# Scores of two heads side by side, and projections in threes, in a stick-breaking attention

## The reference

```python
z = einsum('bhqd,bhkd->bhqk', qb, k) * scale           # scores
strict = key_idx < q_idx                                # keys before the query only
log_one_minus = where(strict, log_sigmoid(-z), 0.0)
suffix = cumsum(log_one_minus, reverse=True) - log_one_minus
w = where(strict, exp(log_sigmoid(z) + suffix), 0.0)
out = einsum('bhqk,bhkd->bhqd', w, v)
```

## Time and profile before

| | |
|---|---|
| time, median of 3 runs | 1234.1 us (1234.05 to 1234.74) |
| the profiled execution's own time | 1235.34 us |
| its span, first to last instruction | 1233.5 us |
| granted TensorE clock, mean | 0.993 of full speed |
| TensorE busy | 1199.7 us, 97% |
| VectorE, ScalarE, GpSimd busy | 57%, 41%, 7% |
| stick-breaking stage | from 101.2 us to about 274 us of the span |

### The profile page before, as it was taken

How to read it: one execution, slowest core, us unless ns; L and a number is a source line. 1 busy time by engine, 2 the same in 40 slices (tenths; PEclk the granted TensorE clock), 3 DMA queues, 4 the chain that set the end, 5 groups by cost and what they waited for, 6 DMA issues and landing times.

```text
span 1233.5 us, 15994 instructions
## 1 busy us (share of the span) xinstructions
PE 1199.7 (97%) x6548; PEld 964.2 (78%) x6548; DVE 701.2 (57%) x1086; ACT 500.9 (41%) x799; POOL 92.3 (7%) x72
## 2 busy tenths in 40 slices
PE   7999999999999999999999999999999999999996
PEld 5787777777777787887777788878888888888885
DVE  6644564359556676457887785364444444433356
ACT  5424434454454455224446545253233223322244
POOL 0390010104000000000000200000000000000000
PEclk9999999999999999999999999999999999999998
DMA  9732322213121343331112101123322222433322
GB/s 370 282 109 71 125 92 84 69 59 101 52 69 52 97 142 98 105 120 45 59 54 84 34 4 36 52 86 103 103 89 100 99 89 98 144 99 100 104 86 71
DMA packets 35593, 118.22 MB, mean 96 GB/s; under 512 B 3936, under 2 KB 6112, under 8 KB 35520
## 3 DMA queue, kind: packets, MB, share of 16 engines
q1 hardware_dynamic: 33024, 111.03, 26.9%
q0 software_dynamic: 1392, 4.72, 1.3%
q10 hardware_dynamic: 1104, 1.45, 0.3%
HBM read 112.99 MB, written 4.19 MB: 95 GB/s over the span
## 4 chain that ended last, share of the span: by engine, by line
PE 85%; DVE 6%; ACT 5%; issue 2%; POOL 0%; DVEq 0%; ACTq 0%
PE pb L650 82%; PE pb L906 1%; DVE wlo L1824 1%; PE pb L736 1%; ACT mP L1539 1%; DVE mnm L2066 1%; DVE xT L1824 1%; ACT whi L1341 1%; ACT Y L1341 1%; DVE mP L2056 1%; DVE junk L1835 0%; PE pb L1068 0%; ACT xT L1560 0%; DVE sp L1824 0%; ACT fv L1341 0%
## 5 line engine op out<-in xcount | busy, mean ns | idle before, releaser
L650 PE MATMUL pb<-hlo,whi 128*128 128x512 f32 (+2 forms) x1056 | 408.9, 394 | 7.1 <-DVE wlo L1824 5.9
L650 PE MATMUL pb<-hhi,wlo 128*128 128x512 f32 (+2 forms) x1056 | 410.8, 389 | 2.6 <-DVE wlo L1824 2.6
L650 PE MATMUL pb<-hhi,whi 128*128 128x512 f32 (+2 forms) x1056 | 409.9, 388 | 0.0
L1824 DVE TENSOR_TENSOR wlo<-raw,whi 128x1024 fp32r<-128x1024 f32 (+1 forms) x178 | 216.1, 1219 | 109.0 <-ACT whi L1341 108.0
L650 PEld LDWEIGHTS pb<-hlo,whi 128*128 128x128 f32 (+1 forms) x1056 | 198.5, 188 | 55.2 <-DVE wlo L1824 8.6
L650 PEld LDWEIGHTS pb<-hhi,wlo 128*128 128x128 f32 (+1 forms) x1056 | 198.1, 188 | 44.0 <-DVE wlo L1824 3.5
L650 PEld LDWEIGHTS pb<-hhi,whi 128*128 128x128 f32 (+1 forms) x1056 | 198.1, 188 | 41.0
L1341 ACT ACTIVATE whi<-raw 128x1024 fp32r<-128x1024 f32 (+1 forms) x178 | 181.5, 1034 | 72.9 <-PE pb L650 67.9
L650 PE MATMUL pb<-alo,whi 128*128 128x512 f32 x176 | 68.5, 389 | 0.0
L650 PE MATMUL pb<-ahi,wlo 128*128 128x512 f32 x176 | 68.5, 389 | 0.0
L650 PE MATMUL pb<-ahi,whi 128*128 128x512 f32 x176 | 68.5, 389 | 0.0
(11 more groups left out here) (363 smaller groups left out, 1632.6 us busy)
## 6 DMA issues: line engine op xcount, KB each, us to landing
raw<-w_all SPq DMA_DIRECT2D x173, 512.0 KB, 3.5
adab<-ada_d SPq DMA_DIRECT2D x12, 512.0 KB, 12.5
raw<-w_all SPq DMA_DIRECT2D x10, 384.0 KB, 3.0
xT<-xn_d SPq DMA_DIRECT2D x4, 512.0 KB, 12.9
gbt<-ada_d SPq DMA_DIRECT2D x4, 512.0 KB, 15.7
ple_scratch<-zs SPq DMA_DIRECT2D x8, 256.0 KB, 12.2
xT<-x_d POOLq DMA_DIRECT2D x8, 256.0 KB, 3.2
out_d<-xT SPq DMA_DIRECT2D x6, 256.0 KB, 2.6
```

The costliest lines, as they stand in the source:

```text
L650: return e.matmul(out, lhs, rhs, start=start, stop=stop, skip_group_check=True)
L1824: return e.tensor_tensor(out, a, b, op)
```

## The change

Scores are computed for a pair of heads at once. `qp` shrinks from 8 slices with zeros to 4 full slices: the even head's queries on partitions 0 to 63, the odd head's on 64 to 127. `sb_qk(pr)` multiplies 64 rows of `kp` with 64 rows of `qp`, one head after the other on different rows and into different banks, and adds the eight masks at the end. GpSimd's zeros and its share of the low part go away; VectorE makes the whole low part, 896 and 256 columns. The order on all engines is written anew: behind the scores of a pair stand three projections, then one behind each suffix, none behind `sb_pv`. The middle one of each group of three uses bank 6. The root and the scaling of the `kv` latent move from F6 to F8, and the four `Silu` of the first gate (with two table loads) move ahead of the three projections of the last pair.

```diff
-        QPE, KPE, SBV = sig("act_qp", range(8)), ...
+        QPE, KPE, SBV = sig("act_qp", range(4)), ...
+        def filler_bank(i):
+            return 6 if i % 5 == 1 else 7
@@ GpSimd
-            def sb_low(h):
-                ...
-                e.tensor_tensor(spl[:, 0:896], sp[:, h % 2, 0:896], fr(sph[:, 0:896]), ALU.subtract).then_inc(SBLO0.sem, 1)
-            for r in range(2):
-                ...
-                e.memset(qp[64 - 64 * r:128 - 64 * r, :, :].rearrange(...)[:, :, r, :], 0.0).then_inc(QZERO.sem, 1)
-            for h in range(8):
-                sb_low(h)
-                if h == 1:
-                    rope_sum("kr", krs[64:96, :], 0)
+            rope_sum("kr", krs[64:96, :], 0)
@@ TensorE
+            def sb_qk(pr):
+                ...
                 for kb in KB_ORDER:
-                    out = sb_out(h, kb)
-                    bank(3 * (h % 2) + BK[kb])
-                    mm(out, kp[:, h // 2, 128 * kb:128 * kb + 128], qp[:, h, 128 * kb:512], kb != 3, False)
-                    t = mm(out[:, 0:128], identB, msB, False, False)
-                t.then_inc(SBQK.sem, 1)
+                    for r in range(2):
+                        bank(3 * r + BK[kb])
+                        rows = slice(64 * r, 64 * r + 64)
+                        mm(sb_out(r, kb), kp[rows, pr, 128 * kb:128 * kb + 128], qp[rows, pr, 128 * kb:512], kb != 3, False)
+                for r in range(2):
+                    for kb in KB_ORDER:
+                        t = mm(sb_out(r, kb)[:, 0:128], identB, msB, False, False)
+                    t.then_inc(SBQK.sem, 1)
...
-            sb_qk(0)
-            next(fa)
             for pr in range(4):
                 h = 2 * pr
-                sb_qk(h + 1)
-                next(fa)
+                sb_qk(pr)
+                for _ in range(3):
+                    next(fa)
                 sb_suffix(h)
-                next(fa)
-                if pr < 3:
-                    sb_qk(h + 2)
                 next(fa)
                 sb_suffix(h + 1)
                 next(fa)
                 sb_pv(pr)
-                if pr < 3:
-                    next(fa)
@@ ScalarE
-                for r in range(2):
-                    copy(qp[64 * r:64 * r + 64, 2 * m + r, :], PB[m][64 * r:64 * r + 64, :], scale=0.125
+                copy(qp[:, m, :], PB[m][:, :], scale=0.125).then_inc(QPE.sem, 1)
...
-            sb_pre(0)
-            sb_pre2(0)
-            next(fa)
             for pr in range(4):
                 h = 2 * pr
-                next(fa)
+                sb_pre(h)
+                sb_pre(h + 1)
+                sb_high(h)
                 if pr == 3:
                     ... (load Silu table, 4 Silu, load the other table)
+                for _ in range(3):
+                    next(fa)
+                sb_high(h + 1)
                 sb_weights(h)
-                ...
                 next(fa)
                 sb_weights(h + 1)
                 next(fa)
@@ VectorE
+            def sb_low(h):
+                V.wait_ge(*SBHI(h))
+                if h:
+                    V.wait_ge(*SBSUF(h - 1))
+                for o, n in ((0, 896), (1024, 256)):
+                    t = tt(spl[:, o:o + n], sp[:, h % 2, o:o + n], fr(sph[:, o:o + n]), ALU.subtract)
+                t.then_inc(SBLO.sem, 1)
...
             for pr in range(4):
                 h = 2 * pr
-                ...
+                sb_pre(h)
+                if pr == 0:
+                    conv("cq", 0)
+                sb_pre(h + 1)
+                sb_max(h)
                 next(fa)
+                sb_max(h + 1)
+                sb_low(h)
                 next(fa)
+                next(fa)
+                sb_low(h + 1)
                 next(fa)
                 next(fa)
```

More of the change, by code:

```diff
@@ L241, in build @@
         with ExitStack() as s1:
-            qp = sb(s1, "qp", [128, 8, S])
+            qp = sb(s1, "qp", [128, 4, S])
             kp = sb(s1, "kp", [128, 4, S])
@@ L433, in build @@
         ZPLE = sig("act_zple", range(8))
[L435 to L439, removed]
+        QPE, KPE, SBV = sig("act_qp", range(4)), sig("dve_kp", range(4)), sig("act_sbv", range(4))
+        SBQK, SBMIN, SBLN, SBMAX, SBHI, SBLO, SBSUF = (
+            sig(n, range(8)) for n in ("pe_sbqk", "dve_sbmin", "act_sbln", "dve_sbmax", "act_sbhi", "dve_sblo", "pe_sbsuf"))
         SBW = sig("act_sbw", [(h, b) for h in range(8) for b in range(3)])
@@ L770, in tensor_program @@
             for m in range(4):
-                free[m] = [QPE(2 * m + 1)]
+                free[m] = [QPE(m)]
             for m in range(4):
@@ L780, in filler_a @@
                 for m in range(5):
-                    project(*(("cq", m) if m < 3 else ("ckv", m - 3)), 128, 7, h1)
-                    free[7] = [CQ(m)]
+                    b = filler_bank(m)
+                    project(*(("cq", m) if m < 3 else ("ckv", m - 3)), 128, b, h1)
+                    free[b] = [CQ(m)]
                     if m == 3:
@@ L791, in filler_a @@
                 yield
-                T.wait_ge(*SS(("c", 4)))
-                sum_squares(6, "kv", ssq[:, :])
                 for m in range(8):
-                    project(*(("sz", m) if m < 4 else ("mz", m - 4)), 128, 7, h1)
-                    free[7] = [ZE(m)]
+                    b = filler_bank(6 + m)
+                    if m == 2:
+                        T.wait_ge(*SS(("c", 4)))
+                        sum_squares(6, "kv", ssq[:, :])
+                    project(*(("sz", m) if m < 4 else ("mz", m - 4)), 128, b, h1)
+                    free[b] = [ZE(m)]
                     yield
                 for m in range(6):
-                    b = 0 if m == 4 else 7
+                    b = filler_bank(14 + m)
                     project("ga", m, 128, b, h1)
@@ L825, in sb_suffix @@
                        sp[:, i, 896:1024], False, False)
-                T.wait_ge(*SBLO0(h))
-                T.wait_ge(*SBLO1(h))
+                T.wait_ge(*SBLO(h))
                 for kb in range(3):
@@ L1446, in filler_a @@
                 yield
-                A.wait_ge(*CQN(2))
-                root(rsb[:, :], 6, 256, "kv")
                 for m in range(8):
                     conv(*(("sz", m) if m < 4 else ("mz", m - 4)))
+                    if m == 2:
+                        A.wait_ge(*CQN(2))
+                        root(rsb[:, :], 6, 256, "kv")
                     yield
@@ L1467, in sb_pre, with sb_high @@
                 e.activation(x, x, ACT.Ln, bias=one_c).then_inc(SBLN.sem, 1)
-            def sb_pre2(h):
+            def sb_high(h):
                 A.wait_ge(*SBMAX(h))
@@ L1476, in sb_weights @@
                 A.wait_ge(*SBSUF(h))
-                A.wait_ge(*SBLO0(h))
-                A.wait_ge(*SBLO1(h))
+                A.wait_ge(*SBLO(h))
                 for b, n in THIRDS:
@@ L1510, in scalar_program @@
             A.wait_ge(*SBPV(3))
-            A.wait_ge(*SBLO0(7))
+            A.wait_ge(*SBLO(7))
             for k in range(5):
@@ L1968, in filler_a @@
                     V.wait_ge(*PLST(7))
-                    e.tensor_copy(zs[:, m, :], PB[7][:, :]).then_inc(ZE.sem, 1)
-                    if m == 0:
+                    e.tensor_copy(zs[:, m, :], PB[filler_bank(6 + m)][:, :]).then_inc(ZE.sem, 1)
+                    if m == 2:
                         latent_normed("kv", 3, 2, V_KN)
@@ L1989, in sb_pre, with sb_max @@
                 t.then_inc(SBMIN.sem, 1)
-            def sb_pre2(h):
+            def sb_max(h):
                 V.wait_ge(*SBLN(h))
@@ L2015, in vector_program @@
                 V.wait_ge(*SBPV(pr))
[L2016 to L2020, removed]
+                e.tensor_copy(qp[:, pr, :], PB[6][:, :]).then_inc(OA.sem, 1)
             for m in range(4):
@@ L2023, in vector_program @@
                 V.wait_ge(*OA(m))
-                tt(zs[:, m, :], zs[:, m, :], qp[:, 2 * m, :], ALU.mult).then_inc(ZA.sem, 1)
+                tt(zs[:, m, :], zs[:, m, :], qp[:, m, :], ALU.mult).then_inc(ZA.sem, 1)
             next(fa)
```

36 lines of the change are left out of this document (4 added, 32 removed).

## The result

The changed kernel took 1245.4 us (median of 5 runs, 1242.6 to 1247.9) beside 1234.7 us of the kernel before (5 runs, 1234.1 to 1236.6): ratio 1.0076, 95% interval 1.0061 to 1.0092, so 10.7 us at the medians, where 8.8 were forecast. Its profiled execution took 1245.4 us, with a span of 1243.6 against 1233.5.

A forecast was written before the change was run, and what follows sets the result against it. TensorE, busy 97% of the span, bounds the kernel. Gains of 14.6 us against costs of 17.6 give 3.0 us more, plus 5.8 for the clock: 8.8 on 1234.1, so 1242.9 us; range 1239 to 1247, for 8 in 10 1236 to 1248.5.

The forecast's parts named there:

- Waits for low parts: TensorE waits for `wlo` ahead of F2 3.28, F3 0.3, F6 4.8, F7 3.28, F9 0.5 and F17 4.2 us.
- the two behind a suffix: Short waits for low parts ahead of F3, 0.3 us, and F9 (`sz 3`), 0.5 us.
- Scores by pairs: Two heads' scores on two halves of rows take 2.79 us instead of 5.04; gain 4 x 2.25 = 9.0 us.
- lost in the first pair for banks 3 to 5: First pair's second head waits for banks until ScalarE's copies of the values leave them: 0.8 us.
- Scores and fewer starts behind other work: Scores by pairs gain 9.0 us; projections starting behind other work fall from 20 to 13, gain 0.6 us.
- Old waits: TensorE's present waits in the stage, about 101 to 281 us, go: 5.0 us gained if none stayed.
- The clock: Granted clock falls behind each long wait, F2, F6, F7 and F17: four times 1.45 us, 5.8 us, bounds 0 and about 12.
- slow first steps: Each projection behind one of the four long waits pays 0.1 us for its first step: 0.4 us.
- VectorE's whole low part: VectorE's low part on all columns, at most 1.6 us twice a pair, behind at least one projection: worth nothing.
- The rival that hoped for a quicker VectorE: VectorE's chain ahead of F2, F6, F7, F17 shorter without GpSimd, each wait 2 us less: 1229.1 us, chance 0.10.
- the one in which the halves run apart: Scores on the two halves of rows don't run together, the 9.0 us are missing: 1251.9 us, chance 0.07.
- The rival with an unchanged clock: The waits come but the granted clock stays: 1234.1 + 3.0 = 1237.1 us, chance 0.14.

The follow-up runs named there:

- second experiment: Changed kernel with ScalarE and VectorE converting two weight chunks ahead everywhere, also where ada chunks lie between: 1227.05 us, ratio 0.9926 to the kernel before.
- third: Changed kernel with the four Silu and their two table loads behind ScalarE's three conversions of the last pair: 1237.1 us, ratio 1.0014 to the kernel before.
- ninth: Changed kernel with ScalarE's first conversion between the two heads' exponentials and logarithms from the second pair on: 1232.75 us, ratio 0.9971 to the kernel before.
- last experiments: Against the kernel with everything that waited mended (1218.0 us): 64-row scores one head after the other, 1225.0 us; zero-padded scores over all 128 rows, 1228.6 us.
- first experiment: Changed kernel with 14, 21, 14 and 18 identity products on TensorE ahead of F2, F6, F7 and F17: 1236.4 us, ratio 1.0011 to the kernel before.
- fourth experiment: Changed kernel with GpSimd again making the first 896 columns of each low part, VectorE the last 256: 1244.1 us, ratio 1.0056 to the kernel before.
- half-filled kernel: Changed kernel with 7, 11, 7 and 9 identity products on TensorE ahead of F2, F6, F7 and F17: 1241.1 us, ratio 1.0044 to the kernel before.
- filled kernel: Same run as the first experiment: changed kernel with identity products on TensorE in the four long waits, 1236.4 us.
- all-in kernel: Changed kernel with two weight chunks ahead, Silu block behind the three conversions, values' projection in banks 2, 5, 6, 7: 1218.0 us, ratio 0.9857 to the kernel before.

## Why the prediction was right, step by step

- **Waits for low parts.** Right in place, releaser and size, six of six: 16.4 us foretold, 16.3 measured in the same count (16.6 if the two behind a suffix also go from start to start). The second experiment shows their cause, the third and ninth the part that ScalarE's order has in F17 and F6.
- **Scores by pairs.** 2.79 us a pair as read from FoX, and 0.75 us lost in the first pair for banks 3 to 5 where 0.8 was foretold. The last experiments split the gain: 1.60 of 2.25 us a pair is the alternation of halves.
- **Scores and fewer starts behind other work.** The third pair, which has no stops in either kernel, takes 238.46 - 200.30 = 38.16 us from scores to scores against 238.48 - 197.90 = 40.58: 2.42 us, times four 9.7, as 9.0 + 0.6 foretold. After, then before:

```profile
200.30 2.43 PE L633 MATMUL pb<-qp,kp 64*128 64x512 f32 x16
...
238.46 2.43 PE L633 MATMUL pb<-qp,kp 64*128 64x512 f32 x16
```

```profile
197.90 1.02 PE L650 MATMUL pb<-qp,kp 128*128 128x512 f32 x2
...
238.48 1.02 PE L650 MATMUL pb<-qp,kp 128*128 128x512 f32 x2
```

- **Old waits.** Right that they go, but too small by 1.2 us. The prediction took them at 5.0 us, the idle time in brackets, and the new long ones from start to start. From start to start the seven old stops are 6.2 us (each stretch less the time that the same work takes without a stop: 2.52 us for scores, 2.79 for a suffix, 2.30 for a product with values).
- **The clock.** Right in kind, all four stops bring it down; mis-sized. The term was four times 1.45 us, 5.8, taken from the stretch of 2.93 us in the earlier trace rows; it measured 9.6, because three of the four stretches at 1.2 GHz lasted about twice as long as that one. That the total came out only 1.9 us over the 8.8 forecast is in part luck: the clock cost 3.8 us more than foretold, the old waits gave 1.2 more, and 1.6 came back far behind the stage. The rule of the Trainium skill (TensorE: Matmul & The Clock Gate, "Why this matters for your kernels"), that idle gaps between bursts bring the clock down, was borne out for all four. The 1.79 us gap at 57.54 alone would have misled: it was one draw, and in the first experiment's execution a gap of that length brought the clock down.
- **The sum.** All from start to start, -9.7 + 0.75 - 6.2 + 16.6 + 9.6 + 0.5 for slow first steps makes 11.55 us for a stage that grew by 11.3. The 0.3 us between weren't traced.
- **VectorE's whole low part** took 1.42 us and cost nothing, as priced. The rival that hoped for a quicker VectorE is refuted by the fourth experiment, and the one in which the halves run apart by the 2.79 us. The rival with an unchanged clock is what the first experiment made. It was worked out as 3.0 us slower than the kernel before. By the ratio it is 1.4 us slower (0.1 to 2.7), and its stage is 170.3 - 168.5 = 1.9 us longer; the old waits of 1.2 us too little account for the difference of the stages.

## What to carry to other kernels

When two steps are moved next to each other, ask what the step between them was hiding: here a copy, a sum and a conversion of 3.28 us in a row, hidden by 2.5 to 3 us of other work. On a kernel in which TensorE is busy 97% of the time, a stop costs its length and then the slow stretch behind it, here about 60% again (9.6 us on 16.3). Mend the look-ahead together with the new order: the order alone gave 1245.4 us and the look-ahead alone 1233.0, both together 1227.1. The last step to 1218.0 took the later Silu block and the free banks as well.

## What was not expected of the hardware

- A stop of 3.1 to 4.5 us was followed by 3.4 to 6.1 us in which products took nearly twice their time, costing 1.65 to 2.9 us each.
- Stops of 1.6 to 2.1 us bring the clock down at one time and not at another. In one execution of the half-filled kernel one of 2.13 us did, while 1.60, 1.60 and 2.11 us, and one of 2.07 us ahead of the stage, did not. At the same place ahead of the stage the clock fell in the filled kernel's execution (1.79 us) and stayed at 1.00 in those of the kernel before (1.79 us) and of the changed one (1.87 us). Ten executions of the half-filled kernel spread over 8 us, with a mean granted clock of 0.988 for the slowest and 0.995 for the fastest; but the kernel before, without long stops in the stage, spread over 4.8 us too (19 runs), and the all-in kernel's four within 1.3.
- Beside a subtraction on GpSimd, one on VectorE takes longer: 2.31 us in place of 1.23 for a weight chunk's low part, 2.08 in place of 0.41 for 256 columns. It cost the kernel next to nothing, since such a meeting was late for TensorE only once, by 0.23 us.
- A product over 64 rows isn't only good for running beside another: two heads in turn took 4.39 us on 64 rows each and 4.84 on 128.
